# The output projection's rows are scaled on GpSimd instead of DVE, next to the variance

## Chip, cores and metric

The kernel runs on one core of a Trainium2 chip. The metric is the device time of one execution in microseconds, the median of several runs. Engines are named as in the profile: PE is TensorE, DVE is VectorE, ACT is ScalarE, POOL is GpSimd, SP issues the big weight loads.

## What is computed

The kernel runs a hybrid layer (state-space and delta-rule mixers) and then two layers of a second block on 512 tokens of width 2048. The place in question is the seam between the two:

```
# end of the first block: y is the mixers' output
o     = y @ w_out
x1    = x + gate * (o * rsqrt(mean(o*o) + EPS) * post_w)
# opening of layer 0 of the second block
h     = x1 * rsqrt(mean(x1*x1) + EPS) * norm_g
proj  = h @ w_in
```

Everything lies transposed: features on the 128 partitions, tokens along the free dimension. A 2048 x 512 matrix is 16 tiles of 128x512, numbered k = 0 to 15. A mean over features is therefore a sum of tiles and then a product with a matrix of ones on TensorE, which leaves the sum on every partition.

## The kernel before, in words

Products in float32 precision are made of three products of rounded parts: a tile is split into a rounded `hi` and the remainder `lo`, and `hi*hi`, `hi*lo`, `lo*hi` are summed in PSUM. Weights come in units of 128x1024 by SP's queue; ACT makes `whi` (L2791), DVE makes `wlo` (L3004, the function `split`), three units ahead of TensorE. Activations are split the same way: ACT writes `u_hi` (L2917), DVE writes `u_lo`.

The output projection runs tile by tile (L2617). After each tile, ACT takes it out of PSUM (`take_out`: its square into `o_sq`, a copy into `res[k]`), and squares it times its gate (`square_gated`); DVE multiplies it with x (`cross_out`), and adds up squares, cross products and gated squares in `o_sum`, `cross_sum`, `gated_sum`. Of the last tile the three results are not added up: they go to TensorE by themselves. So when the last tile is done, `out_sums` multiplies six tiles with ones, two for each sum: `nb` gets the squares (L2631, L2635), `ob` the cross products (L2633, L2640), `tb` the gated squares (L2638, L2642).

From `nb` ACT makes the root `o_rs` = rsqrt(mean(o*o)) by a logarithm (L2941) and an exponential (L2943), each with a load of its table. DVE then makes the variance of x1 from the three sums, without x1 itself, in five operations (`make_var`, L3048 to L3056), and ACT makes its root `x_rs` (L2946, L2948). Meanwhile and after that DVE runs, for every k, `add_out` (L3059: `res[k]` times `o_rs`; drain; L3061: times `gam[k]`, plus `x[k]`, into `x[k]`), `make_u` (L3192: x1 times `norm_g` times `x_rs` into a ring of four tiles) and the remainder `u_lo` (L3196) once ACT has rounded. The order on DVE is written out by hand: after `make_var` comes `add_out(0)`, a weight split, `add_out(1)`; then, in step k, `make_u(k)`, `u_lo(k-1)`, `add_out(k+2)`, and after steps 6 and 10 a pair of weight splits (`LEAD_SPLITS`).

TensorE opens layer 0 with `lead` (L2597): four output tiles side by side (`om`, `sA`, `sB`, `ob`), so that each k gives 12 products as soon as its `u_lo` is there; 192 products for the 16 k. After `lead` it goes on tile by tile (L2580), with the first sum of squares at L2652.

GpSimd issues DMAs here: for each k it waits for `x1_added` and stores x1 (`store_x1`, L2514); after k = 8 it also loads memory keys, values and a bias, and after the last store four small vectors. `res` lies in a room that is used again by those loads.

Of the kernel before, what the change touches and what calls it, by code (L numbers as in the profile page):

```python
# [9 lines left out]
ALU = mybir.AluOpType  # L10
# [4 lines left out]
KT = D // P  # L15
# [2300 lines left out]
def layers(nc, dr, cols, c_lat, ident, rs, x, x_rs, stage, y_loaded, w_loaded):  # L2316
# [71 lines left out]
    with Phase(nc, "lay") as ph:  # L2388
# [20 lines left out]
        res = room[:, 0:8192].rearrange("p (k t) -> p k t", k=KT)  # L2409
        cross_sum, gated_sum, o_rs, var = (room[:, 8192 + 512 * j:8704 + 512 * j] for j in range(4))  # L2410
        o_sum = x_rs
        o_sq, cross, gated = (four[:, j, :] for j in range(3))
# [5 lines left out]
        ones, half = ph.sb("ones", [P, P]), ph.sb("half", [P, P])  # L2418
# [7 lines left out]
        nb, sA, sB, tb, ob, om = (ph.pb(n) for n in ("nb", "sA", "sB", "tb", "ob", "om"))  # L2426
# [5 lines left out]
        eps_ready, lam_sum, lam_exp = ph.sem("eps_ready"), ph.sem("lam_sum"), ph.sem("lam_exp")  # L2432
# [9 lines left out]
        x_loaded, x1_added, x1_stored = [ph.sem(f"x_loaded{j}") for j in range(4)], ph.sem("x1_added"), ph.sem("x1_stored")  # L2442
        g_loaded, g_turned, gam_ready = (ph.sem(n) for n in ("g_loaded", "g_turned", "gam_ready"))
        o_squared, o_taken, o_crossed, o_gated = (ph.sem(n) for n in ("o_squared", "o_taken", "o_crossed", "o_gated"))
        o_added, cross_added, gated_added = (ph.sem(n) for n in ("o_added", "cross_added", "gated_added"))
        o_summed, cross_done, o_logged, o_rs_ready, var_ready, x_rs_ready = (
            ph.sem(n) for n in ("o_summed", "cross_done", "o_logged", "o_rs_ready", "var_ready", "x_rs_ready"))

# [20 lines left out]
        with nc.Block() as block:  # L2469
# [19 lines left out]
            @block.gpsimd  # L2489
            def _(pool):  # L2490
                def load_memory(l):
                    kv = dr.mkvT[l].rearrange("(k p) t -> p k t", p=P)
                    pool.dma_start(mk, kv[:, 0:MH, :]).then_inc(mk_loaded, 16)
                    pool.dma_start(msc, kv[:, MH:2 * MH, :]).then_inc(mv_loaded, 16)

                def load_alibi(g):
                    h = g % DH
                    if g:
                        pool.wait_ge(score_read, 2 * LCH * g)
                    pool.dma_start(alibi, dr.alibi[:, h * ABIAS:(h + 1) * ABIAS]).then_inc(alibi_loaded, 16)  # L2500

                def load_res(l, n):
                    src = dr.x1T if l == 0 else dr.x2T
                    if n < 4:
                        pool.wait_ge(pv_done, LCH * DH * (l + 1))
                    else:
                        pool.wait_ge(added, KT * l + n - 3)
                    pool.dma_start(four[:, n % 4, :], src[n * P:(n + 1) * P, :]).then_inc(res_loaded[n % 4], 16)

                for t, at in ((half, C_HALF), (ones, C_ONES)):  # L2510
                    pool.dma_start(t[:], dr.consts[:, at:at + P]).then_inc(c_loaded, 16)
                def store_x1(k):
                    pool.wait_ge(x1_added, k + 1)
                    pool.dma_start(dr.x1T[k * P:(k + 1) * P, :], x[:, k, :]).then_inc(x1_stored, 16)  # L2514

                pool.dma_start(gacc, dr.gate_sums.rearrange("q p n -> p q n")).then_inc(g_loaded, 16)
                for k in range(KT):
                    store_x1(k)
                    if k == 8:
                        load_memory(0)  # L2520
                        load_alibi(0)
                for n, v in enumerate((dr.lambda_q1_2, dr.lambda_k1_2, dr.lambda_q2_2, dr.lambda_k2_2)):
                    pool.dma_start(lamv[:, n, :], v.rearrange("l e -> (l e)").partition_broadcast(P)).then_inc(lam_loaded, 16)
                for i in range(NQ_ALL + 1):
                    l, j = divmod(i, NU)
                    if i in alibi_at and alibi_at[i] < LAYERS * DH:
                        load_alibi(alibi_at[i])
                    if i in y_at:
                        yl, h = y_at[i]
                        g = yl * DH + h  # L2530
                        if h == 0:
                            pool.wait_ge(x_stored if yl else x1_stored, 16 * KT * max(yl, 1))
                        pool.wait_ge(y_taken, g + 1)
                        pool.wait_ge(tile_a, evac_a[yl, TILES.index(("g", h))])
                        pool.tensor_tensor(x[:, y_slot("d", h), :], ytmp, gate[:, h % 2, :], ALU.mult).then_inc(y_done, 1)
                    if l < LAYERS:
                        if j == U_OUT - 12:
                            for n in range(4):
                                load_res(l, n)
                        if j == U_OUT + 2 and l + 1 < LAYERS:  # L2540
                            pool.wait_ge(conv_done, CT * (l + 1))
                            load_memory(l + 1)
                    for tl, t in evac_at.get(i, ()):
                        if TILES[t][0] == "o":
                            n = TILES[t][1]
                            pool.wait_ge(added, KT * tl + n + 1)
                            dst = dr.x2T if tl < LAYERS - 1 else dr.out
                            pool.dma_start(dst[n * P:(n + 1) * P, :], x[:, n, :]).then_inc(x_stored, 16)
                            if n + 4 < KT:
                                load_res(tl, n + 4)  # L2550
                pool.wait_ge(x_stored, 16 * KT * LAYERS)

            @block.tensor
            def _(pe):
# [73 lines left out]
                def out_sums():  # L2628

                    pe.wait_ge(o_added, KT - 1)  # L2630
                    pe.matmul(nb[:], ones[:], o_sum[:], start=True, stop=False)  # L2631
                    pe.wait_ge(cross_added, KT - 1)
                    pe.matmul(ob[:], ones[:], cross_sum, start=True, stop=False)  # L2633
                    pe.wait_ge(o_squared, KT)
                    pe.matmul(nb[:], ones[:], o_sq, start=False, stop=True).then_inc(o_summed, 1)  # L2635
                    pe.wait_ge(gated_added, KT - 1)
                    pe.wait_ge(gam_ready, 1)
                    pe.matmul(tb[:], ones[:], gated_sum, start=True, stop=False)  # L2638
                    pe.wait_ge(o_crossed, KT)
                    pe.matmul(ob[:], ones[:], cross, start=False, stop=True)  # L2640
                    pe.wait_ge(o_gated, KT)
                    pe.matmul(tb[:], ones[:], gated, start=False, stop=True).then_inc(cross_done, 1)  # L2642
# [101 lines left out]
                for g in range(4, NX):  # L2744
                    n, h = O_UNITS[g]
# [38 lines left out]
            def _(act):  # L2784
# [13 lines left out]
                def take_out(n):  # L2798
                    act.wait_ge(unit_done, O_LAST[n] + 1)
                    act.wait_ge(y_left, KT)  # L2800
                    act.wait_ge(o_added, n)
                    act.activation(o_sq, o_bank(n)[:], ACT.Square).then_inc(o_squared, 1)
                    act.activation(res[:, n, :], o_bank(n)[:], ACT.Copy).then_inc(o_taken, 1)

                def square_gated(n):
                    act.wait_ge(gam_ready, 1)
                    act.wait_ge(o_taken, n + 1)
                    act.wait_ge(gated_added, n)
                    act.activation(gated, res[:, n, :], ACT.Square, scale=gam[:, n:n + 1]).then_inc(o_gated, 1)
# [121 lines left out]
                for g in range(1, NX):  # L2931
                    split(g + LEAD - NX)
                    if g in o_at:
                        take_out(o_at[g])
                    if g in cross_at:
                        square_gated(cross_at[g])
                take_out(KT - 1)
                square_gated(KT - 1)
                act.wait_ge(eps_ready, 1)
                act.wait_ge(o_summed, 1)  # L2940
                act.activation(o_rs, nb[:], ACT.Ln, bias=eps[:, 1:2], scale=1.0 / D).then_inc(o_logged, 1)  # L2941
                act.wait_ge(o_logged, 1)
# [56 lines left out]
            def _(dve):  # L2999
                def split(i):  # L3000

                    g = NX + i
                    dve.wait_ge(hi_ready, g + 1)
                    dve.tensor_tensor(wlo[:, g % SLOTS, :, :], stage[:, g % DEEP, :, :], whi[:, g % SLOTS, :, :].bitcast(F32), ALU.subtract)\  # L3004
                        .then_inc(lo_ready, 1)
# [50 lines left out]
                    dve.tensor_scalar(var, var, EPS, None, ALU.max).then_inc(var_ready, 1)  # L3056

                def add_out(k):
                    dve.tensor_tensor(res[:, k, :], res[:, k, :], o_rs, ALU.mult)  # L3059
                    dve.drain()  # L3060
                    dve.scalar_tensor_tensor(out=x[:, k, :], in0=res[:, k, :], scalar=gam[:, k:k + 1], in1=x[:, k, :], op0=ALU.mult, op1=ALU.add)\  # L3061
                        .then_inc(x1_added, 1)

# [165 lines left out]
                cross_out(KT - 1)  # L3229
                make_var()  # L3230
                add_out(0)
                split(LEAD)
                add_out(1)
                dve.wait_ge(x_rs_ready, 1)
                for k in range(KT + 1):
                    dve.wait_ge(x1_added, min(k + 1, KT))
# [110 lines left out]
```

## Time and profile before

| | us |
|---|---|
| median of 3 runs | 3414.93 |
| the runs | 3413.44, 3414.93, 3420.15 |
| profiled execution, its own time | 3416.97 |
| span of the profile | 3415.2 |
| PE busy | 3280.1 (96%) |
| DVE busy | 1655.6 (48%) |
| ACT busy | 1477.4 (43%) |
| POOL busy | 296.0 (9%) |
| mean granted clock of PE | 0.984 |

The profile is one execution; its times are counted from the span's start. Busy time counts an instruction from its start to its end, so time in which an instruction has started and stands still counts as busy. A line such as L3004 is a line of the kernel. In a row of the timeline the start comes first, then the duration, engine, line, operation, output and inputs, shape, and in brackets the idle time before it and who ended it.

### The profile page before, as it was taken

What the parts mean: (1) busy time and instruction counts of PE and PEld (TensorE: products, weight loads), DVE (VectorE), ACT (ScalarE), POOL (GpSimd) and SP (SyncE); (2) the same over time, 40 slices, a digit from 0 to 9 for tenths busy, and PEclk for the clock granted to TensorE, in tenths of its full rate; (3) what the DMA queues carried; (4) which work ended last, traced back from release to release, by engine and by line L of the source; (5) the groups of instructions that cost most, each with busy time, mean ns of one, the idle gap of its engine ahead of it and who ended that gap; (6) DMA issues with size and microseconds to landing.
All of it is one profiled execution on the core that took longest, in us unless ns stands there. A gap on an engine that the chain in (4) does not pass through costs nothing.

```text
span 3415.2 us, 52416 instructions
## 1 busy us (share of the span) xinstructions
PE 3280.1 (96%) x21470; PEld 2668.9 (78%) x21470; DVE 1655.6 (48%) x2770; ACT 1477.4 (43%) x2386; POOL 296.0 (9%) x311
## 2 busy tenths in 40 slices
PE   8999999999988889898999999999999999999999
PEld 5778888888877878786777777887877777788787
DVE  4655665666534656556544444334344444533432
ACT  4362442344346575333655554223246555522211
POOL 0000320130003423001000000000000000000010
PEclk9999999999998999899999999999999999999999
DMA  9922424434730102333322223334422222233242
GB/s 360 368 73 81 125 85 142 136 93 145 230 109 21 46 27 83 138 99 119 102 76 80 80 80 104 94 98 141 140 89 76 78 80 85 80 105 95 90 149 86
DMA packets 141519, 383.29 MB, mean 112 GB/s; under 512 B 15296, under 2 KB 23616, under 8 KB 141280
## 3 DMA queue, kind: packets, MB, share of 16 engines
q1 hardware_dynamic: 132880, 349.91, 31.7%
q0 software_dynamic: 8400, 30.02, 2.7%
q8 instruction: 171, 2.80, 0.3%
q14 instruction: 68, 0.56, 0.1%
HBM read 350.31 MB, written 29.56 MB: 111 GB/s over the span
## 4 chain that ended last, share of the span: by engine, by line
PE 56%; DVE 1%; ACT 1%; issue 1%; DVEq 0%; POOL 0%; ACTq 0%
PE lay_acc L2580 42%; PE lay_acc L2617 3%; PE lay_sA L2691 1%; PE lay_sB L2617 1%; PE lay_sA L2617 1%; PE lay_ob L2709 1%; PE lay_nb L2652 1%; PE lay_tb L2670 1%; PE lay_om L2580 1%; PE lay_om L2597 0%; PE lay_sA L2597 0%; PE lay_sB L2597 0%; PE lay_om L2719 0%; PE lay_ob L2597 0%; DVEq L3060 0%
## 5 line engine op out<-in xcount | busy, mean ns | idle before, releaser
L2580 PE MATMUL lay_acc<-lay_u_hi,lay_whi 128*128 128x512 f32 x2144 | 853.9, 398 | 0.0
L2580 PE MATMUL lay_acc<-lay_u_hi,lay_wlo 128*128 128x512 f32 x2144 | 836.2, 390 | 0.0
L2580 PE MATMUL lay_acc<-lay_u_lo,lay_whi 128*128 128x512 f32 x2144 | 835.2, 390 | 0.0
L3004 DVE TENSOR_TENSOR lay_wlo<-all_x_sb,lay_whi 128x1024 fp32r<-128x1024 f32 x320 | 400.1, 1252 | 593.7 <-ACT lay_whi L2791 592.9
L2791 ACT ACTIVATE lay_whi<-all_x_sb 128x1024 fp32r<-128x1024 f32 x320 | 337.1, 1055 | 587.7 <-PE lay_acc L2580 415.3
L2580 PEld LDWEIGHTS lay_acc<-lay_u_hi,lay_whi 128*128 128x128 f32 x2144 | 403.4, 188 | 97.8 <-issue 16.5
L2580 PEld LDWEIGHTS lay_acc<-lay_u_hi,lay_wlo 128*128 128x128 f32 x2144 | 402.9, 188 | 86.3
L2580 PEld LDWEIGHTS lay_acc<-lay_u_lo,lay_whi 128*128 128x128 f32 x2144 | 403.6, 188 | 83.3 <-issue 2.9
L924 PE MATMUL proj_lat<-proj_u_hi,proj_whi 128*128 128x512 f32 x816 | 334.0, 409 | 0.9 <-DVE proj_wlo L1176 0.8
L924 PE MATMUL proj_lat<-proj_u_hi,proj_wlo 128*128 128x512 f32 x816 | 321.0, 393 | 0.0
L924 PE MATMUL proj_lat<-proj_u_lo,proj_whi 128*128 128x512 f32 x816 | 320.9, 393 | 0.0
L1046 ACT ACTIVATE proj_whi<-tokens_unit_stage 128x512 fp32r<-128x512 f32 x212 | 132.0, 628 | 391.7 <-PE proj_ctx L926 272.1
L1176 DVE TENSOR_TENSOR proj_wlo<-tokens_unit_stage,proj_whi 128x512 fp32r<-128x512 f32 x208 | 150.7, 729 | 243.9 <-ACT proj_whi L1046 243.0
L924 PEld LDWEIGHTS proj_lat<-proj_u_hi,proj_whi 128*128 128x128 f32 x816 | 153.8, 188 | 39.4 <-issue 6.8
L924 PEld LDWEIGHTS proj_lat<-proj_u_lo,proj_whi 128*128 128x128 f32 x816 | 153.6, 188 | 35.3 <-issue 1.4
L924 PEld LDWEIGHTS proj_lat<-proj_u_hi,proj_wlo 128*128 128x128 f32 x816 | 153.6, 188 | 34.3
L926 PE MATMUL proj_ctx<-proj_u_hi,proj_wlo 128*128 128x256 f32 x432 | 121.0, 280 | 0.0
L926 PE MATMUL proj_ctx<-proj_u_hi,proj_whi 128*128 128x256 f32 x432 | 121.0, 280 | 0.0
L926 PE MATMUL proj_ctx<-proj_u_lo,proj_whi 128*128 128x256 f32 x432 | 120.7, 279 | 0.0
L1749 PE MATMUL gdn_PT<-gdn_Q,gdn_TU 64*64 64x64 f32 x1920 | 90.9, 226 | 16.5 <-DVE gdn_Q L2116 13.8
L1735 PE MATMUL gdn_PT<-gdn_TU,gdn_AT 64*64 64x64 f32 x1920 | 81.9, 226 | 21.4 <-ACT gdn_TU L1859 12.6
L1195 DVE SCALAR_TENSOR_TENSOR proj_obuf<-proj_lat,all_cols,proj_obuf 128x496 f32<-128x496 f32 (+1 forms) x128 | 94.3, 737 | 7.5 <-issue 0.4
(497 smaller groups left out, 5255.9 us busy)
## 6 DMA issues: line engine op xcount, KB each, us to landing
all_x_sb<-units_dram SPq DMA_DIRECT2D x288, 512.0 KB, 3.5
tokens_unit_stage<-in_units_dram SPq DMA_DIRECT2D x212, 256.0 KB, 2.7
front_stage<-in_w_ada_dram SPq DMA_DIRECT2D x64, 512.0 KB, 8.1
front_stage<-in_w_kv_dram SPq DMA_DIRECT2D x32, 512.0 KB, 6.8
tokens_kv_out<-in_w_ada_dram SPq DMA_DIRECT2D x64, 256.0 KB, 3.2
all_x_sb<-out_units_dram SPq DMA_DIRECT2D x32, 512.0 KB, 3.6
all_x_sb<-scr_arow SPq DMA_DIRECT2D x32, 256.0 KB, 4.3
all_x_sb<-in_xT_dram SPq DMA_DIRECT2D x4, 1536.0 KB, 11.0
```

The costliest lines, as they stand in the source:

```text
L924: mm = pe.matmul(banks(t)[0][:], w[:, i % SLOTS, k, :], ut[:, kt, 0:LAT], **at)
L926: mm = pe.matmul(banks(t)[1][:, 0:CTX], w[:, i % SLOTS, k, :], ut[:, kt, LAT:TOK], **at)
L1046: act.activation(whi[:, i % SLOTS, :, :], stage[:, i % DEEP, :, :], ACT.Copy).then_inc(hi_ready, 1)
L1176: dve.tensor_tensor(wlo[:, i % SLOTS, :, :], stage[:, i % DEEP, :, :], whi[:, i % SLOTS, :, :].bitcast(F32), ALU.subtract)\
L1195: op = dve.scalar_tensor_tensor(out=o[:, :, b:w - z], in0=x[:, :, b + off:w - z + off], scalar=conv_cols(t, tap)[0], in1=o[:, :, b:w - z], ...
L1735: mm = pe.matmul(PT[d][q_rows(rows, v), narrow(h)], AT[rows, d, s % 3, block_at(h, rows)], TU[rows, d, s % 2, narrow(h)], start=True, stop ...
L1749: pe.matmul(PT[d][rows, narrow_t(h)], TU[q, d, s % 2, narrow_t(h)], Q[q, d, narrow(h)], start=True, stop=True)
L2580: mm = pe.matmul(bank_of(t)[:], w[:, i % SLOTS, k, :], u[:, kt, :], start=(kt == n == 0), stop=(kt == KT - 1 and n == 2))
L2617: mm = pe.matmul(o_bank(n)[:], w[:, g % SLOTS, k, :], u[:, kt, :], start=(kt == m == 0), stop=(kt == KT - 1 and m == 2))
L2652: pe.matmul(nb[:], mat[:], sq[:, e % 2, :], start=(kind != "x"), stop=True).then_inc(normed, 1)
L2791: act.activation(whi[:, g % SLOTS, :, :], stage[:, g % DEEP, :, :], ACT.Copy).then_inc(hi_ready, 1)
L3004: dve.tensor_tensor(wlo[:, g % SLOTS, :, :], stage[:, g % DEEP, :, :], whi[:, g % SLOTS, :, :].bitcast(F32), ALU.subtract)\
```

## The change

GpSimd takes over the multiplication of `res[k]` with `o_rs`: after the last tile's products have been read and `o_rs` is there, it scales tiles 0 to 3, and from then on tile k+4 before it stores x1's tile k. DVE's `add_out` waits for `o_scaled` and does the rest in one operation, without the drain. `out_sums` sends the last tile's squares right behind the first sum of squares, and the cross sum after that. ACT's wait for the epsilon constants stands before the last tile's squares instead of before the logarithm. On DVE `add_out(1)` comes before the weight split instead of after it.

```diff
 # GpSimd
                 pool.dma_start(gacc, dr.gate_sums.rearrange("q p n -> p q n")).then_inc(g_loaded, 16)
+
+                def scale_out(k):
+                    pool.tensor_tensor(res[:, k, :], res[:, k, :], o_rs, ALU.mult).then_inc(o_scaled, 1)
+
+                pool.wait_ge(o_crossed, KT)
+                pool.wait_ge(o_gated, KT)
+                pool.wait_ge(o_rs_ready, 1)
+                for k in range(4):
+                    scale_out(k)
                 for k in range(KT):
+                    if k + 4 < KT:
+                        scale_out(k + 4)
                     store_x1(k)
                     if k == 8:
                         load_memory(0)
...
 # TensorE, out_sums
                     pe.wait_ge(o_added, KT - 1)
                     pe.matmul(nb[:], ones[:], o_sum[:], start=True, stop=False)
+                    pe.wait_ge(o_squared, KT)
+                    pe.matmul(nb[:], ones[:], o_sq, start=False, stop=True).then_inc(o_summed, 1)
                     pe.wait_ge(cross_added, KT - 1)
                     pe.matmul(ob[:], ones[:], cross_sum, start=True, stop=False)
-                    pe.wait_ge(o_squared, KT)
-                    pe.matmul(nb[:], ones[:], o_sq, start=False, stop=True).then_inc(o_summed, 1)
...
 # ACT
+                act.wait_ge(eps_ready, 1)
                 take_out(KT - 1)
                 square_gated(KT - 1)
-                act.wait_ge(eps_ready, 1)
                 act.wait_ge(o_summed, 1)
                 act.activation(o_rs, nb[:], ACT.Ln, bias=eps[:, 1:2], scale=1.0 / D).then_inc(o_logged, 1)
...
 # DVE
                 def add_out(k):
-                    dve.tensor_tensor(res[:, k, :], res[:, k, :], o_rs, ALU.mult)
-                    dve.drain()
+                    dve.wait_ge(o_scaled, k + 1)
                     dve.scalar_tensor_tensor(out=x[:, k, :], in0=res[:, k, :], scalar=gam[:, k:k + 1], in1=x[:, k, :], op0=ALU.mult, op1=ALU.add)\
                         .then_inc(x1_added, 1)
...
                 make_var()
                 add_out(0)
+                add_out(1)
                 split(LEAD)
-                add_out(1)
                 dve.wait_ge(x_rs_ready, 1)
```

## Rows read from the trace of the kernel before

**Rows 1.** Chain of waits, 1578 to 1600 us: start, duration, what.
```profile
1578.67 0.86 PE lay_nb L2631 x2
...
1585.28 0.69 DVE lay_room L3048
...
1588.35 0.43 DVE lay_room L3056
...
1595.54 0.60 DVE lay_u_lo L3196
```
**Rows 2.** Timeline of PE, layer 0.
```profile
1596.29 0.76 PE L2597 MATMUL lay_om<-lay_u_hi,lay_whi 128*128 128x512 f32 x1 [12.47 <-DVE lay_u_lo L3196]
...
1627.66 0.69 PE L2597 MATMUL lay_om<-lay_u_hi,lay_whi 128*128 128x512 f32 x1 [1.86 <-DVE lay_u_lo L3196]
...
1645.70 1.02 PE L2652 MATMUL lay_nb<-lay_room,lay_ones 128*128 128x512 f32 x2
...
1678.24 0.66 PE L2691 MATMUL lay_sA<-lay_four 64*128 64x512 f32 x1 [1.08 <-issue]
```
**Rows 3.** Windows: length, busy of PE, PEld, DVE, ACT, POOL; clock, DMA share, GB/s.
```profile
1596.30:1600.30 4.00, 4.00 (x10) 3.13 (x11) 3.85 (x7) 0.63 (x1) 0.54 (x1) 0.50 0.33 126
...
1627.70:1631.40 3.70, 3.70 (x9) 2.89 (x10) 3.55 (x6) 0.63 (x1) 0.54 (x1) 0.54 0.71 268
...
1678.24:1684.00 5.76, 5.76 (x25) 4.18 (x26) 2.61 (x6) 5.67 (x7) 0.00 (x0) 1.00 0.35 94
```
**Rows 4.** Timeline of ACT, from the last projected tile on.
```profile
1578.71 0.60 ACT L2802 ACTIVATE lay_four<-lay_sB 128x512 f32<-128x512 f32 x1 [3.71 <-PE lay_sB L2617]
...
1579.88 0.72 ACT L2809 ACTIVATE lay_four<-lay_room,lay_gam 128x512 f32<-128x512 f32 x1
1581.33 1.28 ACT L2941 ACT_TABLE_LOAD   x1 [0.73 <-PE lay_nb L2635]
...
1590.75 0.63 ACT L2948 ACTIVATE stream_x_rs<-stream_x_rs 128x512 f32<-128x512 f32 x1
```
**Rows 5.** Timeline of DVE, in the lead: one step, one pair of splits.
```profile
1598.75 0.68 DVE L3059 TENSOR_TENSOR lay_room<-lay_room 128x512 f32<-128x512 f32 x1
1599.51 0.75 DVE L3061 SCALAR_TENSOR_TENSOR all_x_sb<-lay_room,lay_gam,all_x_sb 128x512 f32<-128x512 f32 x1
1600.17 0.75 DVE L3192 SCALAR_TENSOR_TENSOR lay_four<-all_x_sb,all_cols,stream_x_rs 128x512 f32<-128x512 f32 x1
1600.84 0.68 DVE L3196 TENSOR_TENSOR lay_u_lo<-lay_four,lay_u_hi 128x512 fp32r<-128x512 f32 x1
...
1610.95 2.35 DVE L3004 TENSOR_TENSOR lay_wlo<-all_x_sb,lay_whi 128x1024 fp32r<-128x1024 f32 x2
...
1613.88 0.68 DVE L3196 TENSOR_TENSOR lay_u_lo<-lay_four,lay_u_hi 128x512 fp32r<-128x512 f32 x1
```
**Rows 6.** POOL's groups by line and shape: busy us, mean ns, idle before.
```profile
L2535 POOL TENSOR_TENSOR all_x_sb<-lay_room 128x512 f32<-128x512 f32 x12 | 15.4, 1286 | 473.4 <-DVE lay_room L3136 393.4 <-issue 80.0
...
L2514 POOL DMA_DIRECT2D scr_x1T<-all_x_sb x16 | 8.7, 544 | 228.9 <-DVE all_x_sb L3061 228.9
```
**Rows 7.** Timeline of POOL and DVE at 1803 us.
```profile
1803.92 1.29 POOL L2535 TENSOR_TENSOR all_x_sb<-lay_room 128x512 f32<-128x512 f32 x1 [38.51 <-DVE lay_room L3136]
...
1804.51 1.78 DVE L3004 TENSOR_TENSOR lay_wlo<-all_x_sb,lay_whi 128x1024 fp32r<-128x1024 f32 x1 [0.68 <-ACT lay_whi L2791]
```
**Rows 8.** Timeline of POOL and DVE at 1271 us.
```profile
1271.56 2.95 POOL L1664 TENSOR_TENSOR gdn_attn<-all_x_sb,gdn_kq 128x512 f32<-128x512 f32 x2 [7.03 <-ACT gdn_kq L1845]
...
1272.17 4.09 DVE L2172 TENSOR_TENSOR gdn_o<-gdn_o,gdn_var 128x512 f32<-128x512 f32 x4
```
**Rows 9.** Timeline of POOL and DVE at 401 us (`proj_s` lies in PSUM).
```profile
401.50 0.68 DVE L1281 TENSOR_TENSOR all_x_sb<-all_x_sb,mixers_tq 128x512 f32<-128x512 f32 x1
401.75 1.59 POOL L873 TENSOR_TENSOR all_x_sb<-all_x_sb 128x512 f32<-128x512 f32 x1 [9.62 <-DVE all_x_sb L1274]
...
402.26 0.69 DVE L1283 TENSOR_TENSOR all_x_sb<-all_x_sb,proj_s 128x512 f32<-128x512 f32 x1
```

More of the change, by code:

```diff
@@ L2444, in layers @@
         o_squared, o_taken, o_crossed, o_gated = (ph.sem(n) for n in ("o_squared", "o_taken", "o_crossed", "o_gated"))
-        o_added, cross_added, gated_added = (ph.sem(n) for n in ("o_added", "cross_added", "gated_added"))
+        o_added, cross_added, gated_added, o_scaled = (ph.sem(n) for n in ("o_added", "cross_added", "gated_added", "o_scaled"))
         o_summed, cross_done, o_logged, o_rs_ready, var_ready, x_rs_ready = (
```

## Prediction

> **What bounds the kernel now.** The page first: PE is busy 96% of the span, so only a stretch where TensorE stands still, or a stretch that makes it start late, can give or cost anything. The diff touches one such stretch, the end of the output projection and the opening of layer 0, so I read the chain of waits there. It leaves TensorE after the sums over partitions, runs through ACT's root of the projected rows, through DVE's five variance operations, and then stays on DVE until the first rounded-off remainder `u_lo` is ready [rows 1]. The timeline of TensorE then shows two waits for `u_lo`: 12.47 us before product group k=0 and 1.86 us before k=10, and the lead's last product is followed by the next work at 1645.70 [rows 2]. Between these waits TensorE needs 12 products of 0.227 us, 2.72 us, per k, and DVE 2.69 us per k: multiply and drain 0.76, gamma-add 0.66, `make_u` 0.67, `u_lo` 0.60 [rows 5]. They are nearly level, and what DVE spends on the weight splits (2.27 us per pair, after k=6 and after k=10 [rows 5]) tips it: the second pair is what makes k=10 late.
>
> A wait also costs clock. After the 12.47 us the granted clock is 0.50 for ten products (half, 1.2 of 2.4 GHz; 0.43 us each, 2.0 us lost), after the 1.86 us it is 0.54 over 3.7 us; a wait of 1.08 us elsewhere leaves it at 1.00 [rows 2, 3]. The 72 products from 1627.66 to 1645.70 took 18.04 us where 72 x 0.227 = 16.34: the restart costs 1.7 us. Behind the lead all is paced by TensorE again, so the change of the total is the change of that 1645.70.
>
> **Part 1, square's sum ahead of the cross sum, and the eps wait.** ACT is done with its last gated square at 1579.88 + 0.72 = 1580.60 and then stands 0.73 us for the sum [rows 4]. One place earlier is worth 0.86 us [rows 1]: the sum lands about 1580.4, and its input, the square of 1578.71 + 0.60 = 1579.31 [rows 4], is there when TensorE comes to it at 1579.5. So ACT goes on at 1580.60: **-0.73 us** on the root. The eps wait costs and gives nothing: whether or not ACT's table load can now go ahead of the wait, ACT is busy until 1580.60 and the sum is there by then. The cross sums still finish at 1583.8, before the root (1584.5).
>
> **Part 2, what DVE is rid of.** 16 multiplies with their drain, 0.76 us each [rows 5]. Three of them stand before the first `u_lo` (k = 0, 1, 2): **-2.28 us**; from there one per k. Putting `add_out(1)` ahead of the split swaps two pieces of DVE work that both stand before the first `make_u`: nothing, unless the root of the variance is late (checked below).
>
> **Part 3, what GpSimd takes.** The same product of two SBUF tiles, 128x512, takes GpSimd 1.286 us against 0.68, and a store's issue 0.54 us [rows 5, 6]. Its round of one multiply, one issue and some 0.3 us of waiting, 2.1 us, is under TensorE's 2.72; it starts four k ahead. With nothing else it would be hidden, the three loads that it issues at k=8 included. Behind GpSimd's new wait for the root stand only the stores, which wait for DVE's adds anyway.
>
> But the two engines do not run side by side. A GpSimd multiply began at 1803.92, and a DVE subtraction that takes 1.22 us alone (two take 2.35, overlapping by 0.08) took 1.78 beside it: it got going at 1805.07, 0.14 us before the multiply's end [rows 5, 7]. The other way round, a multiply behind a DVE operation took 1.59, that is, began when the operation was 0.12 us from its end [rows 9]. And they take turns: two multiplies against four DVE operations back to back, 2.95 us instead of 2.5, and 4.09 instead of 4 x 0.60 + 0.08 = 2.48 [rows 8]. Of these 1.61 us, 0.53 is the rest of the multiply under way (1271.56 + 1.28 - 0.14 - 1272.17), and **one whole turn of GpSimd costs DVE 1.08 us**. That is more than the 0.76 which DVE saves. A DVE operation with its second operand in PSUM runs free beside a multiply, 0.69 us [rows 9].
>
> Now the turns. Multiply 0 runs from 1584.6 beside the two variance operations that read PSUM: free. Multiply 1, from 1585.90, stops the third (ready 1586.10) for 0.94 us; multiply 2, behind a drain, stops the fourth for 0.92. The fifth (L3056) has one SBUF operand; I take it as free, by the nearest row (the PSUM one), so the rest of multiply 3, 0.56 us, falls on `add_out(0)`. Bounds for that choice: 0 and 0.35 us more. Multiplies 4, 5, 6 stop `add_out(1)`, `make_u(0)` and `make_u(1)`: 3 x 1.08. Sum 5.66 us.
>
> The Trainium skill (SBUF — State Buffer, "Who interferes with whom") says that a `tensor_scalar` can run in a two-port mode and then also shuts GpSimd out. No row here shows one beside a multiply; by that rule the start comes 0.35 us later, and the total would be 3418.8.
>
> The root of the variance: 2.60 us lie between the last variance operation's end (1588.78) and ACT's last exponential (1591.38) [rows 1, 4]; with that operation's end at 1589.9 it is there at 1592.5, and DVE comes to `make_u(0)` at 1593.9: not late.
>
> **The sum.** First `u_lo`: -0.73 - 2.28 + 5.66 = **+2.65**, TensorE starts at 1598.9. For k = 1 to 6 each k has one turn: 6 x (1.08 - 0.76) = +1.92, so k=6 is 4.57 late: 1613.88 + 0.68 + 4.57 = 1619.1 [rows 5]. TensorE, six groups of 2.72 and the slow start of 2.0 on, wants it at 1617.3: a new wait of 1.8 us, and with it a restart at half clock, 1.7 us. For k = 7 to 10 three multiplies are left: -4 x 0.76 + 3 x 1.08 = +0.20; and DVE, without a multiply before the second pair of splits, comes about 0.45 us too soon for ACT's half of them. So k=10 is 5.2 late, 1632.85. TensorE wants it at 1619.2 + 4 x 2.72 + 1.7 = 1631.8 and waits 1.0 us, which leaves the clock up [rows 2, 3]. The end: 1632.85 + 16.34 = 1649.2 against 1645.70, **+3.5 us**. Bounds: TensorE's own pace from k=6 on gives no less than +2.4; if the 1.0 us wait drops the clock, +5.2.
>
> Stores and the small loads behind them come some 3 us later and end in no wait on this path: DVE finishes adding well before the lead's end.
>
> The profiled execution takes 3416.97 (span 3415.2 and 1.8 around it) and would take 3420.5; it lies 2.0 over the median 3414.93, which becomes **3418.4 us** (+0.10%). What a measurement of this kernel can tell from no change is about 0.2%, 6.8 us: this forecast is "no change".
>
> **Rivals.**
> 1. *GpSimd is hidden after all* (the other sign): DVE is not held up. The start is then -0.73 - 2.28, with 0.23 us of waiting for the variance's root, -2.8; DVE at 1.93 us per k runs ahead, so the 1.86 us at k=10 and its 1.7 us restart go: -6.3, 3408.6 us, just inside 0.2%. For it: GpSimd's own round of 2.1 us. Against it: [rows 7, 8], DVE operations with both operands in SBUF, as all of these. 0.12.
> 2. *The multiply itself slows while DVE stands in line* (slower): 1.59 us was seen [rows 9], which I read as 0.31 of waiting. If it is slower running, all of multiplies 1 to 15 cost DVE 0.31 more, 4.65 us by k=10; the wait there grows to 1.9, the clock drops: 5.2 + 4.65 = +9.85, 3424.8 us. It passes 0.2% from some 0.11 us per multiply with the drop (1.6 us over fifteen turns). Against it: the 2.95 us pair fits 1.28 and a hand-over [rows 8]. 0.12.
> 3. *DVE keeps the port and GpSimd starves*: then DVE waits for `o_scaled` instead; the port's time per k, 1.93 + 1.08, is the same, and so is the total within 1 us. It is counted with the forecast.
>
> **How the numbers follow.** Forecast with its bounds (+2.4 to +5.2: 3417.3 to 3420.1) 0.72, rival 1 0.12, rival 2 0.12, the rest 0.04 for sizes beyond. Half of rival 1 falls past -0.2%: faster 0.06. Rival 2 and 0.04 of the forecast's upper end with the scatter of medians (the three runs lie within 6.7 us): slower 0.16. Same 0.78. The range leaves out rival 1 and what lies above rival 2: 3410 to 3425.
>
> **What would show it.** Right: DVE operations at L3052, L3054, L3061 and L3192 of 1.6 to 1.8 us, each with a GpSimd multiply in front; GpSimd multiplies of about 1.6; rounds of 3.0 us on DVE until k=9 and 1.9 to 2.0 after; the L2941 table load at 1580.6; TensorE starting about 1599 and waiting at k=6 and, shorter, at k=10. Wrong: DVE operations still 0.68 to 0.75 beside the multiplies, or one wait of TensorE only; and if a wait of 1 us already brings half clock, the upper bound holds.

## Result, and the profile after

The kernel with the change takes 3424.64 us (median of 12 runs, 3420.92 to 3427.93) against 3417.77 for the kernel before (12 runs, 3413.08 to 3422.65): ratio 1.0026, interval 1.0018 to 1.0035. The medians lie 6.9 us apart and the ratio makes it 8.9 (6 to 12 by its interval), where +3.5 was forecast. The time itself lies just inside the predicted range, under the 3425 that rival 2 had put there, and the kernel before came out 2.8 us higher than the 3414.93 that the forecast started from.

The profiled execution takes 3420.98, the second fastest of the twelve, and has the highest mean clock (0.985; the others 0.982 to 0.984): the other runs had less clock than this trace shows. Its span is 3419.2, only 4.0 over the span before; but there the last projected tile comes out of PSUM at 1573.66 instead of 1578.71 [rows 4], 5.05 us earlier, in a stretch that the change does not touch. From that row to the span's end it is 1845.5 us against 1836.5: +9.0, near the ratio's figure, though this is one execution of each. All that follows is counted from the start of that evacuation.

The table gives the stage in every kernel profiled; those below "after" are the experiments of the next section. "Root" is the end of the exponential that makes `o_rs`; `u_lo` is the end (start plus duration) of the remainder of that k; the lead's end is the start of the matmul that follows it (`lay_nb`); round is the distance of two `u_lo` between k=0 and 5; in brackets TensorE's wait there. Each row is one execution.

| us from the evacuation's start | root | u_lo 0 | round | u_lo 6 | u_lo 10 | lead's end |
|---|---|---|---|---|---|---|
| before | 6.54 | 17.43 | 2.69 | 35.85 | 48.89 (1.86) | 66.99 |
| forecast for after | 5.81 | 20.08 | 3.01 | 40.4 (1.8) | 54.1 (1.0) | 70.5 |
| after | 5.83 | 22.93 | 3.42 | 46.10 (3.03) | 59.57 (0.78) | 76.10 |
| wait between store and multiply | 5.83 | 20.37 | 2.96 | 40.48 (1.79) | 54.01 (0.77) | 70.52 |
| stores issued by ACT | 5.83 | 21.32 | 3.02 | 41.97 (1.39) | 54.62 (0.78) | 71.15 |
| two half stores | 5.83 | 20.89 | 3.29 | 45.06 (4.69) | 58.25 (0.41) | 74.76 |
| sums alone | 5.83 | 16.71 | 2.69 | 35.14 | 48.18 (1.79) | 64.72 |
| multiplies ahead on DVE | 5.83 | 14.41 | 2.66 | 30.34 | 43.25 | 65.51 |
| the same, lambda loads early | 5.83 | 14.40 | 2.66 | 30.33 | 43.22 | 62.75 |
| before, lambda loads early | 6.54 | 17.42 | 2.69 | 35.84 | 48.89 (1.79) | 65.47 |

Timeline of ACT of the kernel after, from the last projected tile on, which answers to [rows 4]:

```profile
1573.66 0.60 ACT L2813 ACTIVATE lay_four<-lay_sB 128x512 f32<-128x512 f32 x1 [3.76 <-issue]
...
1574.82 0.72 ACT L2820 ACTIVATE lay_four<-lay_room,lay_gam 128x512 f32<-128x512 f32 x1
1575.56 1.28 ACT L2952 ACT_TABLE_LOAD   x1
...
1578.86 0.63 ACT L2954 ACTIVATE lay_room<-lay_room 128x512 f32<-128x512 f32 x1
```

The 0.73 us in front of the logarithm's table load are gone, and the root is 0.71 earlier. The timelines of GpSimd and DVE, in order of time; DVE's lines are the last four of the five variance operations, the add L3071, the weight split L3015, `make_u` L3202 and `u_lo` L3206; L2519 is the multiply on GpSimd, L2514 the issue of a store:

```profile
1579.66 7.23 POOL L2519 TENSOR_TENSOR lay_room<-lay_room 128x512 f32<-128x512 f32 x5 [188.21 <-ACT lay_room L2954]
1580.28 0.69 DVE L3061 TENSOR_TENSOR lay_room<-lay_room,lay_ob 128x512 f32<-128x512 f32 x1
1581.05 1.65 DVE L3063 SCALAR_TENSOR_TENSOR lay_room<-lay_room 128x512 f32<-128x512 f32 x1
1582.78 1.60 DVE L3065 TENSOR_TENSOR lay_room<-lay_room,all_rs 128x512 f32<-128x512 f32 x1
1584.45 1.33 DVE L3067 TENSOR_SCALAR lay_room<-lay_room 128x512 f32<-128x512 f32 x1
1585.70 2.41 DVE L3071 SCALAR_TENSOR_TENSOR all_x_sb<-lay_room,lay_gam,all_x_sb 128x512 f32<-128x512 f32 x2
1587.75 0.59 POOL L2514 DMA_DIRECT2D scr_x1T<-all_x_sb  x1 [0.85 <-DVE all_x_sb L3071]
1588.03 4.50 DVE L3015 TENSOR_TENSOR lay_wlo<-all_x_sb,lay_whi 128x1024 fp32r<-128x1024 f32 x1
1588.36 1.27 POOL L2519 TENSOR_TENSOR lay_room<-lay_room 128x512 f32<-128x512 f32 x1
1589.56 0.59 POOL L2514 DMA_DIRECT2D scr_x1T<-all_x_sb  x1
1590.17 1.27 POOL L2519 TENSOR_TENSOR lay_room<-lay_room 128x512 f32<-128x512 f32 x1
...
1594.15 0.58 POOL L2514 DMA_DIRECT2D scr_x1T<-all_x_sb  x1 [2.71 <-DVE all_x_sb L3071]
1594.44 2.15 DVE L3206 TENSOR_TENSOR lay_u_lo<-lay_four,lay_u_hi 128x512 fp32r<-128x512 f32 x1
1594.76 1.28 POOL L2519 TENSOR_TENSOR lay_room<-lay_room 128x512 f32<-128x512 f32 x1
...
1616.00 0.76 POOL L2494 DMA_DIRECT2D lay_room<-scr_mkvT  x1
1616.57 2.59 DVE L3202 SCALAR_TENSOR_TENSOR lay_four<-all_x_sb,all_cols,stream_x_rs 128x512 f32<-128x512 f32 x1
1616.76 0.55 POOL L2500 DMA_DIRECT2D lay_room<-alibi_dram  x1
1617.32 1.27 POOL L2519 TENSOR_TENSOR lay_room<-lay_room 128x512 f32<-128x512 f32 x1
```

What is to be read here: an operation's duration less what it takes alone is called its hold. The split of 1588.03 takes 1.22 alone and took 4.50: held 3.28 us, until 1591.31, which is 0.13 before the end of the *second* multiply. In between lie the first multiply's end and a store's issue, and DVE did not get going there, where it had got going between two multiplies before the stores began (the operations of 1581.05 to 1585.70). The `u_lo` of 1594.44 started 0.32 us before the multiply did, beside the store's issue, and was yet held until 0.13 before the multiply's end: 1.47 us, not 1.08. The `make_u` of 1616.57 started 0.75 before its multiply, beside the loads, and was held 1.85, until 0.17 before the multiply's end.

The timeline of TensorE after, for [rows 2]: its wait, and the matmul after the lead.

```profile
1596.74 0.77 PE L2608 MATMUL lay_om<-lay_u_hi,lay_whi 128*128 128x512 f32 x1 [17.87 <-DVE lay_u_lo L3206]
...
1619.82 0.50 PE L2608 MATMUL lay_om<-lay_u_hi,lay_whi 128*128 128x512 f32 x1 [3.03 <-DVE lay_u_lo L3206]
...
1633.29 0.50 PE L2608 MATMUL lay_om<-lay_u_hi,lay_whi 128*128 128x512 f32 x1 [0.78 <-DVE lay_u_lo L3206]
...
1649.76 0.59 PE L2663 MATMUL lay_nb<-lay_room,lay_ones 128*128 128x512 f32 x1
```

And the windows behind the 3.03 and the 0.78 us, with the columns of [rows 3]: the granted clock was 1.00 behind both.

```profile
1619.82:1623.00 3.18, 3.05 (x12) 2.17 (x12) 3.18 (x3) 0.63 (x1) 1.92 (x2) 1.00 1.05 382
1633.29:1649.72 16.43, 16.43 (x72) 13.62 (x73) 11.46 (x22) 6.22 (x11) 3.75 (x7) 1.00 0.56 154
```

### The profile page after: what moved, and what is told of

It is laid out like the page before. It is cut to its first block, busy times and chain, and to the rows that moved or that the text cites. A ratio compares the mean times of both kernels' runs of the same rounds, so it can differ in the third digit from the quotient of the medians.

```text
span 3419.2 us, 52401 instructions
## 1 busy us (share of the span) xinstructions
PE 3278.1 (96%) x21470; PEld 2665.4 (78%) x21470; DVE 1664.5 (49%) x2754; ACT 1477.7 (43%) x2386; POOL 317.3 (9%) x327
## 4 chain that ended last, share of the span: by engine, by line
PE 50%; DVE 2%; ACT 1%; issue 1%; DVEq 0%; POOL 0%; ACTq 0%
PE lay_acc L2591 42%; PE lay_sA L2702 1%; PE lay_ob L2720 1%; PE lay_nb L2663 1%; PE lay_tb L2681 1%; PE lay_om L2591 1%; DVE lay_u_lo L3206 1%; PE lay_om L2608 0%; PE lay_sA L2608 0%; PE lay_om L2730 0%; PE lay_sB L2608 0%; PE lay_ob L2608 0%; DVE lay_wlo L3015 0%; DVE lay_four L3202 0%; DVE lay_u_lo L3211 0%
## 5 line engine op out<-in xcount | busy, mean ns | idle before, releaser
L3015 DVE TENSOR_TENSOR lay_wlo<-all_x_sb,lay_whi 128x1024 fp32r<-128x1024 f32 x320 | 403.4, 1262 | 594.6 <-ACT lay_whi L2802 593.8
```

## Experiments

Two theories stood after the result. T1: a store's issue directly in front of a multiply lets GpSimd keep DVE out from the issue on, so that a turn costs more than a multiply alone. T2: a multiply itself costs DVE about 1.5 us in this stage, issue or not. Each of the first two experiments takes the issue from in front of the multiply in another way.

**A wait between store and multiply** (after, GpSimd's loop):

```diff
                 for k in range(KT):
+                    if k == 1:
+                        pool.wait_ge(lo_ready, NX + LEAD + 1)   # DVE's split
+                    if k == 2:
+                        pool.wait_ge(u_made, 1)
+                    if 3 <= k and k + 4 < KT:
+                        pool.wait_ge(u_left, k - 2)
                     if k + 4 < KT:
                         scale_out(k + 4)
                     store_x1(k)
```

> The changed kernel with one wait more on GpSimd in each round: between the store of x1's tile and the next multiply it waits for a later piece of DVE's work, so that the store's issue is over when the multiply starts. Nothing else moves. Measure: the stretch from the last projected tile's evacuation to the end of the lead, 67.0 us before, 76.1 after. Theory 1 (a store's issue directly in front of a multiply lets GpSimd hold the shared port from the issue on, and keeps DVE from its turn between two multiplies): no DVE operation over 1.9 us, about 1.1 us lost per turn, rounds of 3.0 us in place of 3.42, the split of 4.5 us back to 1.2 to 2.3; stretch 70 to 71.5 us; ratio to the kernel before about 1.001. Theory 2 (a multiply costs DVE 1.5 us in the lead, whatever stands in front of it): rounds still 3.4, stretch 75.5 to 77, ratio 1.0026.

Measured: 3418.27 us, ratio 1.0010 (1.0001 to 1.0019); lead's end 70.52, rounds 2.96. GpSimd and DVE in one round:

```profile
1599.14 0.58 POOL L2514 DMA_DIRECT2D scr_x1T<-all_x_sb  x1
1599.67 0.68 DVE L3212 TENSOR_TENSOR lay_u_lo<-lay_four,lay_u_hi 128x512 fp32r<-128x512 f32 x1
...
1600.44 1.72 POOL L2519 TENSOR_TENSOR lay_room<-lay_room 128x512 f32<-128x512 f32 x1 [0.71 <-DVE lay_u_lo L3212]
1600.94 1.77 DVE L3208 SCALAR_TENSOR_TENSOR lay_four<-all_x_sb,all_cols,stream_x_rs 128x512 f32<-128x512 f32 x1
```

The multiply now waits for DVE (1.72 instead of 1.28: it stands in line behind the add), and DVE is held 1.77 - 0.74 = 1.03 us. That is the forecast's turn (1.08), and the whole row of the table is within 0.3 us of the forecast's. Six multiplies hold DVE before the first `u_lo`, as the forecast had counted.

**Stores issued by ACT** (after): GpSimd keeps the wait for the add, without which the multiplies would run ahead, and issues nothing.

```diff
 # GpSimd, for each k
-                    store_x1(k)
+                    pool.wait_ge(x1_added, k + 1)
 # ACT, after it has rounded tile k
+                    act.wait_ge(x1_added, k + 1)
+                    act.dma_start(dr.x1T[k * P:(k + 1) * P, :], x[:, k, :]).then_inc(x1_stored, 16)
```

> The changed kernel with the 16 stores of x1 issued from ACT's queue; GpSimd keeps its waits for x1_added and does only the multiplies and the loads. Theory 1 (the store's issue in front extends the hold): multiplies follow a plain wait, turns of 1.1 us, rounds of about 3.0 us, stretch 70 to 71.5 us, ratio about 1.001; only the multiply behind the three loads may still hold longer. Theory 2 (1.5 us per multiply in the lead by itself): rounds 3.4, stretch 75.5 to 77. If ACT's issues delay its rounding, u_hi comes later by their length and both numbers rise by some tenths.

Measured: 3419.23 us, ratio 1.0008 (0.9999 to 1.0017); lead's end 71.15, rounds 3.02. The same split, and a later `u_lo`:

```profile
1591.15 3.91 POOL L2519 TENSOR_TENSOR lay_room<-lay_room 128x512 f32<-128x512 f32 x2 [0.63 <-DVE all_x_sb L3073]
1591.65 2.28 DVE L3017 TENSOR_TENSOR lay_wlo<-all_x_sb,lay_whi 128x1024 fp32r<-128x1024 f32 x1
...
1599.34 1.72 POOL L2519 TENSOR_TENSOR lay_room<-lay_room 128x512 f32<-128x512 f32 x1 [1.29 <-DVE all_x_sb L3073]
1599.85 1.76 DVE L3208 TENSOR_TENSOR lay_u_lo<-lay_four,lay_u_hi 128x512 fp32r<-128x512 f32 x1
```

With no issue between two multiplies DVE gets its turn: the split is held 1.06 instead of 3.28, `u_lo` 1.08 instead of 1.47. T2 falls with both runs. Here GpSimd is not held back, and a seventh multiply comes in before the first `u_lo`, as in the kernel after: that is why this row is 1.24 us behind the forecast there, and 0.65 at the lead's end.

**Two half stores in front of each multiply** (after): each store of 512 columns as two of 256, with the later waits on `x1_stored` counting two for each tile (left out here).

```diff
 def store_x1(k):
     pool.wait_ge(x1_added, k + 1)
-    pool.dma_start(dr.x1T[k * P:(k + 1) * P, :], x[:, k, :]).then_inc(x1_stored, 16)
+    for h in range(2):
+        pool.dma_start(dr.x1T[k * P:(k + 1) * P, h * 256:h * 256 + 256], x[:, k, h * 256:h * 256 + 256]).then_inc(x1_stored, 16)
```

> The changed kernel with each store of x1 cut in two halves by columns, so that two issues stand in front of each multiply. Theory 1: the hold grows with what stands in front, by 0.3 to 0.6 us per turn: the DVE operation that meets it takes 2.4 to 2.8 us in place of 2.15, rounds 3.7 to 4.0, stretch 79 us or more. Theory 2: rounds 3.42 as before, stretch 76.

Measured: 3423.07 us in one run; lead's end 74.76, rounds 3.29. Neither theory had this.

```profile
1592.38 1.13 POOL L2515 DMA_DIRECT2D scr_x1T<-all_x_sb  x2 [0.85 <-DVE all_x_sb L3072]
1592.67 1.21 DVE L3016 TENSOR_TENSOR lay_wlo<-all_x_sb,lay_whi 128x1024 fp32r<-128x1024 f32 x1
1593.53 1.48 POOL L2520 TENSOR_TENSOR lay_room<-lay_room 128x512 f32<-128x512 f32 x1
...
1598.22 1.12 POOL L2515 DMA_DIRECT2D scr_x1T<-all_x_sb  x2 [0.85 <-DVE all_x_sb L3072]
1598.51 0.68 DVE L3207 TENSOR_TENSOR lay_u_lo<-lay_four,lay_u_hi 128x512 fp32r<-128x512 f32 x1
1599.11 2.09 DVE L3072 SCALAR_TENSOR_TENSOR all_x_sb<-lay_room,lay_gam,all_x_sb 128x512 f32<-128x512 f32 x1
1599.36 1.28 POOL L2520 TENSOR_TENSOR lay_room<-lay_room 128x512 f32<-128x512 f32 x1
...
1619.85 0.76 POOL L2494 DMA_DIRECT2D lay_room<-scr_mkvT  x1
1619.88 1.80 DVE L3203 SCALAR_TENSOR_TENSOR lay_four<-all_x_sb,all_cols,stream_x_rs 128x512 f32<-128x512 f32 x1
1621.18 1.63 POOL L2520 TENSOR_TENSOR lay_room<-lay_room 128x512 f32<-128x512 f32 x1
```

`u_lo`, begun beside the first issue 0.85 us before the multiply, ran free (0.68); the add, begun 0.25 before it, was held 1.35. The split of 1592.67, begun 0.86 before its multiply, ran free too (1.21), and this multiply, which began when the split had 0.35 us left, took 1.48 instead of 1.28. So the second issue lengthens nothing, and T1 is right only in part: what counts is where the DVE operation begins. In the four kernels with multiplies on GpSimd, those begun 0.09 to 0.75 us before a multiply that had an issue directly in front of it were held until near its end; those begun 0.85 or 0.86 before it were not.

One row fits neither: the `make_u` of 1619.88 began 1.30 us before its multiply, beside the issues of the loads, was held 1.06 and ran at 1620.94, in front of the multiply, which then took 1.63. No multiply was under way while it was held.

In rounds, 1.93 us of DVE work (2.69 less the multiply and drain, 0.76) plus the hold, as a mean over the five rounds, gives every figure of the table with multiplies on GpSimd: 1.93 + 1.49 = 3.42, + 1.36 = 3.29, + 1.03 = 2.96, + 1.09 = 3.02.

**The sums alone** (before, with the new order in `out_sums` and ACT's earlier wait for the constants; the multiplies stay on DVE):

```diff
 # TensorE, out_sums
-                    pe.wait_ge(cross_added, KT - 1)
-                    pe.matmul(ob[:], ones[:], cross_sum, start=True, stop=False)
                     pe.wait_ge(o_squared, KT)
                     pe.matmul(nb[:], ones[:], o_sq, start=False, stop=True).then_inc(o_summed, 1)
+                    pe.wait_ge(cross_added, KT - 1)
+                    pe.matmul(ob[:], ones[:], cross_sum, start=True, stop=False)
...
 # ACT's wait as in the change
```

> The first half of the change alone: last square's sum ahead of the cross sum and the wait for the constants moved, multiplies left on VectorE. Both theories say the same here, since no GpSimd work stands in the stage: the root 5.83 us after the start of the last projected tile's evacuation (before 6.54), the first u_lo 0.7 earlier than before (16.7 against 17.4), rounds of 2.7, the lead's end 0.7 earlier (66.3 against 67.0). Should the end come out at 67 or later with the root at 5.83, the root's gain is lost inside the stage, and the cost of the GpSimd half would be 0.7 us smaller than the 9.8 I count for it.

Measured: 3412.67 us, ratio 0.9991 (0.9982 to 1.0000). Root 5.83, every `u_lo` 0.71 earlier, as expected; but the lead's end is 64.72 where 66.3 was expected, 2.27 earlier than before. The other 1.56 us are clock, lost in the profiled execution of before and not in this one; the ratio's interval (0 to 6 us) does not tell 0.7 from 2.3. TensorE first:

```profile
1623.09 0.50 PE L2597 MATMUL lay_om<-lay_u_hi,lay_whi 128*128 128x512 f32 x1 [1.79 <-DVE lay_u_lo L3196]
...
1639.58 1.02 PE L2652 MATMUL lay_nb<-lay_room,lay_ones 128*128 128x512 f32 x2
```

And the window behind its wait:

```profile
1623.10:1626.80 3.70, 3.70 (x16) 3.06 (x17) 3.55 (x6) 0.64 (x1) 0.54 (x1) 1.00 0.71 271
```

The wait is as long as before (1.79 against 1.86), yet the clock is 1.00 behind it where it was 0.54 [rows 3], and the 72 products take 16.49 us instead of 18.04.

**The multiplies ahead on DVE** (the sums alone, and each multiply issued one step ahead of its add on DVE itself, signalled by a semaphore instead of a drain; `u_lo(k)` follows in the same step):

```diff
+def scale_out(k):
+    if k < KT:
+        dve.tensor_tensor(res[:, k, :], res[:, k, :], o_rs, ALU.mult).then_inc(o_scaled, 1)
 def add_out(k):
-    dve.tensor_tensor(res[:, k, :], res[:, k, :], o_rs, ALU.mult)
-    dve.drain()
+    dve.wait_ge(o_scaled, k + 1)
...
 # after make_var: scale_out(0), scale_out(1), add_out(0), split(LEAD); then for each k
+    make_u(k); add_out(k + 1); u_lo(k); scale_out(k + 2); splits after k = 6 and k = 10
```

> No multiply on GpSimd: the kernel before with the square's sum and the eps wait moved, and the multiplies on DVE one step ahead of their adds, so that a semaphore takes the place of the drain; and make_u, then the next add, then u_lo of the same tile, which brings the first u_lo forward. Both theories leave DVE's operations at 0.68 to 0.75 us here. From the rows of before: root 0.7 us earlier, first u_lo 5.0 instead of 7.4 us behind the variance, rounds 2.56, at most 0.8 us of waiting at k=11 and no restart at half clock; stretch 61 to 62 us, 5 to 6 us less than before, ratio 0.9983 to 0.9986. Rival: the lead is held by something else (ACT's splits, the wait for unit_done), stretch 65 us or more and no difference.

Measured: 3414.61 us, ratio 0.9995 (0.9986 to 1.0004). The first `u_lo` comes at 14.41 and the lead's last product is out at 62.2, though the rounds are 2.66 instead of the expected 2.56 and TensorE waits 1.67 us at k=11 instead of at most 0.8. But then TensorE stands idle: the end is 65.51 instead of 61 to 62, and the expected ratio (0.9983 to 0.9986) did not come. The rival's figure came (65 or more), with another holder than the ones it named. GpSimd, DVE and TensorE:

```profile
1635.81 0.54 POOL L2523 DMA_DIRECT2D lay_lamv<-in_lambda_k_dram  x1
...
1640.30 0.49 DVE L3283 TENSOR_TENSOR lay_lamp<-lay_lamv 128x128 f32<-128x128 f32 x2 [2.64 <-DMA lay_lamv<-in_lambda_k_dram]
...
1643.48 1.19 PE L2652 MATMUL lay_nb<-lay_room,lay_ones 128*128 128x512 f32 x1 [3.36 <-ACT lay_room L2815]
```

The gain went into a new wait: the four lambda vectors, issued by GpSimd behind the last store, land 4.47 us after the start of the last issue; DVE stands 2.64 us for them, ACT's exponential of lambda stands behind DVE, and the square that TensorE wants behind that. Behind the 3.36 us TensorE's clock was 0.63 over 4.5 us, which costs again.

**The same with the lambda loads early**, and **the kernel before with the lambda loads early** as a control:

```diff
                     if k == 8:
                         load_memory(0)
                         load_alibi(0)
+                        # the four lambda loads, moved here from behind the loop
```

> The earlier run with the multiplies one step ahead on VectorE and no drain, and the four loads of the lambda vectors issued by GpSimd behind the k=8 loads instead of behind the last store of the projection. Theory A (what ate that run's gain was the wait for these loads: they landed 4.47 us after their last issue, the small product waited 2.64 us for them on VectorE, ScalarE's square behind it, TensorE 3.36 us behind that): the matmul after the lead starts 62 to 63 us after the stage's start (65.5 with late loads, 67.0 before), TensorE's wait there under 0.6, and 4 to 5 us are won on the kernel before (ratio 0.9985 to 0.9990). Rival B (the loads only came last by the profile; splits of VectorE and ScalarE would hold the matmul anyway): a wait of 2 us or more stays there and the end stays at 65 or later. Rival C: the end comes at 62 to 63, and the next wait, for the evacuation of the tiles after the lead, gives it back within the following 10 us, ratio 0.9995 as before.

> Control for the last run: the kernel before with the four lambda loads alone moved behind the k=8 loads. In the kernel before, VectorE waited 1.89 us for these loads but TensorE showed no idle time at the lead's end. Theory A (these loads matter only once the lead ends earlier): no change, lead's end at 67.0 as before, ratio 0.9997 to 1.0003. Rival (the loads cost the kernel before too, through the splits that VectorE and ScalarE do late behind them): 0.5 to 1.5 us won after the lead, ratio 0.9996 or below.

Measured for the first: 3412.44 us, ratio 0.9987 (0.9978 to 0.9996), the only kernel here whose interval lies wholly under 1. TensorE:

```profile
1624.62 0.50 PE L2597 MATMUL lay_om<-lay_u_hi,lay_whi 128*128 128x512 f32 x1 [0.61 <-DVE lay_u_lo L3248]
...
1639.17 1.10 PE L2652 MATMUL lay_nb<-lay_room,lay_ones 128*128 128x512 f32 x2 [0.61 <-ACT lay_room L2815]
```

Theory A holds in the stage: the lead ends at 62.75, 2.76 us earlier than with late loads and 4.24 earlier than before, of which 1.5 are the clock that the profiled execution of before lost at k=10. Some of it is given back at once (rival C in part): the logarithm's table load behind it starts at 66.44 against 69.52 before, 3.08 earlier; what took the 1.16 us was not tried.

Measured for the control: 3412.44 us, ratio 0.9992 (0.9983 to 1.0001), the same median as the kernel above: the runs do not tell the two apart, nor the sums alone (3412.67), and what the reordering is worth is read from the stage only (62.75 against the control's 65.47, 2.7 us). Every `u_lo` is where it was before, but the lead ends 1.52 us earlier, again by the clock. TensorE first:

```profile
1626.63 0.50 PE L2597 MATMUL lay_om<-lay_u_hi,lay_whi 128*128 128x512 f32 x1 [1.79 <-DVE lay_u_lo L3196]
...
1643.15 1.02 PE L2652 MATMUL lay_nb<-lay_room,lay_ones 128*128 128x512 f32 x2
```

And the window behind its wait:

```profile
1626.65:1630.35 3.70, 3.70 (x16) 3.06 (x17) 3.55 (x6) 0.63 (x1) 0.54 (x1) 1.00 0.64 247
```

So theory A's lead end of 67.0 did not come, and neither did the rival's gain behind the lead: the logarithm's table load starts 67.99 us after the stage's start, 1.53 earlier than before, as the lead's end is. The interval of the ratio takes in both theories. The loads moved nothing that reached TensorE in this trace; the 1.5 us are the clock, which fell behind the 1.86 us wait of before and not behind this 1.79.

## Why the prediction was wrong

**What held.** The root came 0.71 us earlier (forecast 0.73). DVE and GpSimd do not run side by side, and DVE loses more by a turn than its own multiply cost: rival 1 is out. The holds of the third and fourth variance operations are 0.96 and 0.91 (forecast 0.94 and 0.92). TensorE's long waits behind the first are at k=6 and k=10, the second 0.78 us with the clock up, as forecast (1.0); between them there are short ones of 0.34 to 0.51, since a round of 3.42 is longer than TensorE's 2.72. From `u_lo` 10 on it takes 16.53 us to the lead's end, near the forecast's 16.34. And the price of a turn is right where no issue stands directly in front of a multiply: 1.03 with the wait in between, 1.09 with the stores on ACT, forecast 1.08. With the wait, which also holds GpSimd to the six turns that were counted, the whole stage is: first `u_lo` 20.37 against 20.08, `u_lo` 10 54.01 against 54.1, end 70.52 against 70.5, ratio 1.0010 (1.0001 to 1.0019) against +0.10%.

**The step that failed** is "one whole turn of GpSimd costs DVE 1.08 us", used for all multiplies of the lead. The rows that it came from have no DMA issue between the multiplies [rows 8]; in the changed kernel a store's issue stands directly in front of every multiply from the sixth on. I priced the issue as 0.54 us of GpSimd's own time, off the path. It works on DVE: with it a turn costs 1.47 to 1.5 us, and where two multiplies follow each other with one issue between, DVE gets no turn between them. The sign that I had named, multiplies of about 1.6 us that stand in line behind DVE, is there without the issue (1.70 to 1.75 in the first two experiments) and gone with it (1.27 to 1.32). Before the first `u_lo`, by DVE's rows (duration less the time alone), the holds are 0.96 + 0.91 + 0.90 + 1.00 + 3.28 + 1.47 = 8.52, against 5.66 forecast: +2.86, and the first `u_lo` is 2.85 late to the forecast. The terms of that: the split 3.28 instead of two turns, 2.16 (+1.12); a seventh multiply that comes in before the first `u_lo` (+1.47; this count was short whatever the price, since with the stores on ACT a seventh came in too, at 1.07); the fifth variance operation and the adds (+0.26). For k = 1 to 6, five rounds have 1.49 instead of 1.08 (+2.05), and the `make_u` behind the loads of k=8 has 1.85 (+0.77). From there to k=10 it is 0.2 less than forecast. Sum at k=10: +5.5 on +5.2, which is the 10.68 measured.

**L3056 as free** was the wrong choice too. Its `tensor_scalar` (L3067 after) took 1.33 instead of 0.43 [rows 1], held 0.90 us, where the forecast had put 0.56 on the add behind it: +0.34, the 0.35 that it gave as its bound. The next multiply stood in line behind it in turn, 1.44 us instead of 1.27:

```profile
1585.45 1.44 POOL L2519 TENSOR_TENSOR lay_room<-lay_room 128x512 f32<-128x512 f32 x1
```

The Trainium skill (SBUF — State Buffer, "Who interferes with whom") says that this form can shut GpSimd out by a two-port mode. This trace agrees that each waits for the other, with those numbers. It moves little here: less 0.08 by which the adds were held shorter than a turn, it is the +0.26 above.

**The restart at k=6** did not come: 3.03 us of waiting, and the clock at 1.00 behind it where I had 1.7 us for a wait of 1.8. That hid nothing at the end, since k=10 waits for DVE, which is later still. In the same way the 1.86 us wait of before had cost it clock in its profiled execution and did not in two other kernels with nearly that wait (1.79). Without that loss the lead ends at 65.5, as in the control, and the change costs 10.6 us there by the profiles. How often it falls in the unprofiled runs stays open; the ratio is an average over them.

**Rival 2** named the right time (3424.8) by luck, for a reason that is not there: the multiply did not slow, it took 1.27 to 1.32 behind its issues. It was DVE that was held from before the multiply's start.

What stays open is how the issue does it. An issue by itself holds nothing: in the five kernels without multiplies on GpSimd, `before` among them, every DVE operation of 512 columns from the first `u_lo` to the lead's end took its time alone, 0.68 to 0.76 us, beside stores and loads too. So it takes an issue and a multiply behind it; that GpSimd, with nothing to wait for, claims what the two engines share for the next multiply while the issue is still under way would fit the holds begun 0.09 to 0.75 us before a multiply, but not the `make_u` of 1619.88 of the half stores, and it is not shown. No run here had another instruction than a DMA issue in front of the multiply.

## What to carry to other kernels

Moving an operation from DVE to GpSimd pays only where DVE is not busy with operands that all lie in SBUF: here each 0.76 us that DVE was rid of came back as 1.03 to 1.5 us of holds. A price for such a turn must be read from rows with the same neighbours on GpSimd's queue; a DMA issue directly in front of a GpSimd operation is not free for DVE, and a wait between them, or another queue for the DMAs, brought back 5.0 to 5.6 us of the 9.1 by which the lead ended later. When a lead is shortened, look at what lands at its end: against the control (65.47), which lost no clock at k=10, the reordered lead ended at 65.51 with late loads and at 62.75 with early ones, so all of the 2.7 us showed only when the four small loads behind it were issued earlier. And when the end of a stage moves by 1.5 us, look at the clock behind its waits before giving it to the edit.

## What the runs showed of the hardware

- A DVE operation begun 0.09 to 0.75 us before a GpSimd multiply that stands directly behind a DMA issue was held until 0.13 to 0.18 us before the multiply's end; behind multiply, issue, multiply it was held 3.28 us through both. Beside issues that are not directly in front of a multiply DVE ran at its time alone (two splits took 2.35 us at 1614.30 of the kernel after, beside a store and two loads), with one exception, the `make_u` held 1.06 us beside two loads at 1619.88 of the half stores.
- Beside a multiply, the two variance operations that read PSUM took 0.69 us, as without one; the `tensor_scalar` with its one operand in SBUF was held 0.90.
- TensorE's clock did not fall by the length of the wait alone. Behind waits for `u_lo` in the lead it was at 1.00 after 3.03 (after), 1.79 (twice), 1.67 and 1.39 us, and near half (0.54 to 0.57 over 3.7 us) after 1.86 (before), 1.79 (the wait between store and multiply) and 4.69 us (half stores). Behind waits of some 1.8 us both came, so a term of 1.5 to 1.7 us can be in one execution and not in the next. The window of the kernel with the wait between store and multiply, behind its 1.79 us:

```profile
1617.60:1621.30 3.70, 3.70 (x10) 2.95 (x11) 3.70 (x5) 0.63 (x1) 3.00 (x3) 0.57 1.01 381
```
